# Expert stage of a two-block network: scatter, gather and turning at a change of expert, in one unit or in three

## The chip, the cores and the metric

The kernel is written in Bass and runs on one core of one Trainium2 chip. The metric is the device time of one execution in microseconds (us). The kernel before took 3509.97 us in the median of 3 runs (3504.43 to 3512.90). The engines are named as in the profile: PE (TensorE; PEld its weight loads), DVE (VectorE), ACT (ScalarE), POOL (GpSimd), SP (SyncE, which issues the weight transfers).

## The reference

The reference runs a block of depth 2 with neighbourhood attention, a bidirectional RWKV-7 and a convolution side by side, and then a second block of depth 2. Only one part of it matters here, the mixture of experts in the second layer of the first block: 256 tokens of width 1024, 8 SwiGLU experts of hidden width 3584, and each token goes to the two experts with the largest router logits, weighted by the softmax of the two.

```python
def _swiglu(h, w_gate, w_up, w_down):
    return (jax.nn.silu(h @ w_gate) * (h @ w_up)) @ w_down

    logits = (xt @ router).astype(jnp.float32)
    top_logit, top_e = lax.top_k(logits, TOP_K)
    gates = jax.nn.softmax(top_logit, axis=-1)
    ...
    y = jnp.zeros_like(xt).at[s_tok].add(yb[dest] * s_gate[:, None].astype(xt.dtype))
```

Everything is float32.

## The kernel before, in words

**Units.** The weights are cut into parts of 128 x 2048 float32 (1 MB). SP loads them, in the order of their use, into a ring of 6 slots; the load of a part waits until the part six before it has been used (`x_used`). An expert has 14 units of 256 hidden columns. A unit `U` takes three parts: two for its gate and up product, one for its down product. Float32 products are made of three matmuls: each operand is split into a high part (rounded, fp32r) and a low part (the rest). The high half of a weight part is made by ACT (`split`, line 1914), the low half by DVE (`split`, line 1984), which waits for ACT's; PE waits for DVE's (`wl_ok`). ACT has three buffers for high halves.

**The body of a unit** works on two units at once. On PE: first half of the product of unit U+1 (line 1828, 12 matmuls of 512 columns), two transposes of unit U's hidden values (`turn`, line 1836), second half of the product of U+1 (line 1828, 12), `down` of U (line 1849, 12, summed over the whole expert in banks 4 and 5). On ACT: silu of U (line 1932), split, split, the high half of the turned hidden values (line 1938), split. In the first unit of an expert the finished sums of the last expert are copied out between the two splits (`sums_out`, line 1927). On DVE: the product of silu and up (`hid`, line 1999), split, split, the low half of the turned hidden values (line 2003), split. Each engine works strictly in its written order; the order between engines is set by counting semaphores.

**A change of expert.** Tokens are picked by matmuls with one-hot matrices. For expert e there are four pieces of work:
- `choose(e)`, DVE (lines 1962 and 1964): builds the two one-hot matrices, `pick_` for gathering and `send` (with the gates) for scattering, 128 x 128 each for two token tiles.
- `gather(e)`, PE (line 1861): 16 float32 products of 128 columns (32 matmul records) into banks 6 and 7; ACT copies them out as the high half `xg_high` (line 1918), DVE makes the low half `xg_low` (line 1989).
- the turning of `send` on PE (line 1866): two transposes into bank 6, once DVE's subtraction has released it (`xcop`); ACT copies them to `sent` (line 1921).
- `scatter(e)`, PE (line 1876): 8 products of 256 columns from the expert's sums `ysb` through `sent` into banks 6 and 7, in four steps; `add(e)`, DVE (line 1973), adds each step to the tokens, and steps 2 and 3 wait for the adds of 0 and 1.

In `over_units` the first unit of an expert is unrolled, then come all four pieces (`static_part`), then 6 trips of a loop over two units, then one unrolled unit. So PE does unit 0, `scatter(e-1)`, `gather(e+1)`, the turning of `send`, unit 1. ACT does unit 0, the copies of gather and of `send`, unit 1. DVE does unit 0, `choose(e+1)`, `add(e-1)`, the subtraction, unit 1. Expert 0 has no scatter before it, expert 7 no gather. The whole is wrapped in a loop over passes; the tokens of these inputs need one pass.

Of the kernel before, what the change touches and what calls it, by code (L numbers as in the profile page):

```python
# [28 lines left out]
RING = 6  # L29
# [129 lines left out]
def build(nc, parts, xt_in, ct_in, con_in, par1_in, par2_in, lora_in, gate2_in, router_in, bias_in,  # L159
# [1456 lines left out]
    def experts(l, normed):  # L1616
# [134 lines left out]
        met, go = S("pass_met"), S("pass_go")  # L1751
        N, n_units = N_EXP * FFE_UNITS, FFE_UNITS
        base = stream["put"] - stream["skew"]
        trips = (n_units - 2) // 2
        pair_bank, turn_bank = (lambda U: bank(U % 2)), (lambda U: bank(2 + U % 2))
        pair_of = lambda U: 3 * U + 1 if U else 2
        down_of = lambda U: 3 * U + 5 if U < N - 1 else 3 * N
        assert trips * 2 + 2 == n_units and 3 * n_units % RING == 0

        def passes_of(eng):  # L1760
            return eng.value_load(passes[0:1, 0:1], min_val=1, max_val=2)
# [15 lines left out]
        @block.sync  # L1777
        def _(sp):
            sp.wait_ge(S("phase_met").h, 4 * phase["n"])
            sp.wait_ge(used.h, stream["put"])  # L1780
            with sp.Fori(0, passes_of(sp)) as p:
                def load(n, i=None, wait_for=None):

                    if wait_for is not None:
                        sp.wait_ge(x_used.h, wait_for)
                    src = parts[base + n, :, :] if i is None else \
                        parts[bass.ds(i * RING + (base + n), 1), :, :].rearrange("a p n -> p (a n)")
                    sp.dma_start(slots[:, n % RING, :], src).then_inc(x_loaded[n % RING].h, 16)
                for n in range(2):
                    load(n)  # L1790
                for e in range(N_EXP):
                    n0 = 2 + 3 * n_units * e
                    for n in range(n0, n0 + 3):
                        load(n, None, n - RING + 1 if n >= RING else None)
                    with sp.Fori(0, trips) as i:
                        for n in range(n0 + 3, n0 + 9):
                            load(n, i, i * RING + (n - RING + 1))
                    for n in range(n0 + 3 * (n_units - 1), n0 + 3 * n_units - (2 if e == N_EXP - 1 else 0)):
                        load(n, None, n - RING + 1)
                leave(sp, p)  # L1800

        def over_units(eng, e, body, static_part):


            body(e * n_units, 0, 1)
            static_part(e)
            with eng.Fori(0, trips) as i:
                for j in range(2):
                    body(e * n_units + 1 + j, i, trips)
            body((e + 1) * n_units - 1, 0, 1)  # L1810

        @block.tensor
        def _(pe):
            with pe.Fori(0, passes_of(pe)) as p:
                def take(n, i):
                    pe.wait_ge(wl_ok.h, i * RING + (n + 1))
                    return high[:, n % 3, :], low_slots[:, n % RING, :]

                def product(U, n, i, which):

                    e = (U // n_units) % 2
                    wh, wl = (v3(w, KT // 2) for w in take(n, i))
                    if which == 0:
                        pe.wait_ge(ac.h, i * 2 + (U + 1))
                    for j in range(KT // 2):
                        k = which * (KT // 2) + j
                        for g, (x, w) in enumerate(((xg_high[e], wh), (xg_high[e], wl), (xg_low[e], wh))):
                            mm = pe.matmul(pair_bank(U), x[:, k, :], w[:, j, :],  # L1828
                                           start=k == 0 and g == 0, stop=k == KT - 1 and g == 2)
                    mm.then_inc(x_used.h, 1)  # L1830

                def turn(U, i):

                    pe.wait_ge(hp.h, i * 2 + (U + 1))
                    for j in range(2):
                        mm = pe.transpose(turn_bank(U)[:, j * P:(j + 1) * P], hid[:, U % 2, j * P:(j + 1) * P],
                                          C("ident"))
                    mm.then_inc(ht.h, 1)

                def down(U, n, i, times):  # L1840
                    u = U % n_units
                    wh, wl = (v3(w, 2) for w in take(n, i))
                    pe.wait_ge(ac.h, i * 2 + (U + 3))
                    if u == 0 and U:
                        pe.wait_ge(summed.h, U // n_units)
                    for j in range(2):
                        for half in range(2):
                            for g, (h, w) in enumerate(((hid_high, wh), (hid_high, wl), (hid_low, wh))):
                                mm = pe.matmul(bank(4 + half), h[:, U % 2, j * P:(j + 1) * P],  # L1849
                                               w[:, j, half * 512:(half + 1) * 512],  # L1850
                                               start=times == 1 and u == 0 and j == 0 and g == 0,
                                               stop=times == 1 and u > 0 and j == 1 and g == 2, skip_group_check=True)
                    mm.then_inc(x_used.h, 1)

                def gather(e):
                    pe.wait_ge(picked.h, e + 1)
                    if e >= 2:
                        pe.wait_ge(added.h, 4 * (e - 1))
                    for k in range(KT):
                        for tt in range(2):  # L1860
                            mm = pe.matmul(bank(6 + k // 4)[:, (k % 4) * P:(k % 4 + 1) * P], htok[:, tt, k * P:(k + 1) * P],  # L1861
                                           pick_[e % 2][:, tt, :], start=tt == 0, stop=tt == 1)
                    mm.then_inc(gathered.h, 1)
                    pe.wait_ge(xcop.h, e + 1)
                    for tt in range(2):
                        mm = pe.transpose(bank(6)[:, tt * P:(tt + 1) * P], send[e % 2][:, tt, :], C("ident"))
                    mm.then_inc(turned.h, 1)

                def scatter(e):
                    pe.wait_ge(summed.h, e + 1)  # L1870
                    pe.wait_ge(tcop.h, min(e + 2, N_EXP))
                    for f in range(4):
                        if f >= 2:
                            pe.wait_ge(added.h, 4 * e + f - 1)
                        for m in range(2 * f, 2 * f + 2):
                            mm = pe.matmul(bank(6 + f % 2)[:, (m % 2) * LAT:(m % 2 + 1) * LAT], ysb[:, m * P:(m + 1) * P],
                                           sent[e % 2], start=True, stop=True)
                        mm.then_inc(scat.h, 1)

                gather(0)  # L1880
                product(0, 0, 0, 0)
                product(0, 1, 0, 1)

                def body(U, i, times):
                    n = 2 + 3 * U
                    if U < N - 1:
                        product(U + 1, n, i, 0)
                        turn(U, i)
                        product(U + 1, n + 1, i, 1)
                        down(U, n + 2, i, times)  # L1890
                    else:
                        turn(U, i)
                        down(U, n, i, times)

                def own_part(e):
                    if e:
                        scatter(e - 1)
                    if e + 1 < N_EXP:
                        gather(e + 1)
                for e in range(N_EXP):  # L1900
                    over_units(pe, e, body, own_part)
                scatter(N_EXP - 1)
                leave(pe, p)

        @block.scalar
        def _(act):
            with act.Fori(0, passes_of(act)) as p:
# [8 lines left out]
                def gathered_out(e):  # L1916
                    act.wait_ge(gathered.h, e + 1)
                    act.activation(xg_high[e % 2].rearrange("p k s -> p (k s)"), banks[:, 6 * 512:8 * 512], ACT.Copy)\
                        .then_inc(xh_ok.h, 1)
                    act.wait_ge(turned.h, e + 1)  # L1920
                    act.activation(sent[e % 2], bank(6)[:, 0:LAT], ACT.Copy).then_inc(tcop.h, 1)

# [15 lines left out]
                    act.activation(hid_high[:, U % 2, :], turn_bank(U)[:, 0:256], ACT.Copy).then_inc(hh.h, 1)  # L1938
                    split(3 * U + 5, i)

                def own_part(e):
                    if e + 1 < N_EXP:
                        gathered_out(e + 1)
                gathered_out(0)
                for m in range(3):
                    split(m, 0)
                for e in range(N_EXP):
# [5 lines left out]
        def _(dve):  # L1953
            keyed = S("key_moved")
            with dve.Fori(0, passes_of(dve)) as p:
# [48 lines left out]
                                      ALU.subtract).then_inc(ac.h, 1)  # L2004
                    split(3 * U + 5, i)

                def own_part(e):
                    if e + 1 < N_EXP:
                        choose(e + 1)
                    if e:  # L2010
                        add(e - 1)
                    if e + 1 < N_EXP:
                        gathered_low(e + 1)
                for e in range(N_EXP):
                    over_units(dve, e, body, own_part)
# [458 lines left out]
```

## Time and profile before

| | |
|---|---|
| median of 3 runs | 3509.97 us |
| profiled execution | 3507.41 us, span 3505.6 us |
| PE busy over the span | 3069.0 us (88%) |
| DVE, ACT busy | 2121.2 us (61%), 1555.0 us (44%) |
| mean granted TensorE clock | 0.918 |
| expert units | first silu at 1710.0, last at 2749.1 us |
| DVE waiting for ACT's split, line 1984 | 103.0 us in 207 waits |
| PE waiting for DVE before line 1866 | 19.0 us in 8 waits |

In the rows below the times of an execution are counted from the start of the span. A row of a timeline gives start, length, engine, line, operation, what it writes and reads, how many instructions are merged in it, and in brackets how long its engine was idle before it and who ended that. Matmuls are pipelined, so the rows of PE overlap somewhat; distances from start to start are safer than lengths. The instructions of ACT and DVE overlap by about 0.1 us in the same way.

### The profile page before, as it was taken

Reading aid. Unit: us, or ns where it says so; the run is one execution under the profiler, and the core shown is the slowest. Engines: PE = TensorE matmul, PEld = TensorE weight load, DVE = VectorE, ACT = ScalarE, POOL = GpSimd, SP = SyncE. Lnnn points to the kernel's source line nnn. Section 1 sums busy time; section 2 is a strip of 40 time slices with the busy share of each in tenths; the row PEclk is TensorE's granted clock in tenths of the full one; section 3 lists DMA queues with packets and bytes.
Section 4 is the critical chain, followed back from the end, with each engine's and each line's share of the span. In section 5 each row is a group of like instructions: output and inputs, shape, how many; then the busy total and the mean of one; then the engine's idle time right before and its main releaser. Section 6 shows DMA issues by size and latency. Waiting matters only on the chain.

```text
span 3505.6 us, 55996 instructions
## 1 busy us (share of the span) xinstructions
PE 3069.0 (88%) x23354; PEld 2555.7 (73%) x23354; DVE 2121.2 (61%) x2470; ACT 1555.0 (44%) x1810; POOL 0.2 (0%) x4
## 2 busy tenths in 40 slices
PE   6998499699998894775799999999999789998999
PEld 3863277489998761665687787787788667996699
DVE  3365522554445366225588888788888645764576
ACT  2223321334334234112576676676677524453453
POOL 0000000000000000000000000000000000000000
PEclk9996699899999997888899999999999878998799
DMA  6210065235454210000598898798899422542253
GB/s 257 84 60 0 19 219 193 85 132 186 170 183 151 101 49 6 2 3 1 215 369 314 312 371 312 305 371 312 313 370 351 194 84 93 184 172 97 74 190 122
DMA packets 86197, 616.06 MB, mean 176 GB/s; under 512 B 9592, under 2 KB 11264, under 8 KB 12032
## 3 DMA queue, kind: packets, MB, share of 16 engines
q1 hardware_dynamic: 82656, 601.92, 45.8%
q10 hardware_dynamic: 3360, 11.50, 0.9%
q8 instruction: 142, 2.33, 0.3%
q14 instruction: 39, 0.32, 0.0%
HBM read 612.33 MB, written 1.05 MB: 175 GB/s over the span
## 4 chain that ended last, share of the span: by engine, by line
PE 76%; DVE 14%; PEld 3%; ACT 3%; issue 1%; DMA 1%; PEldq 1%; ACTq 0%; DVEq 0%; POOLq 0%
PE banks L1828 17%; PE banks L983 14%; PE banks L635 10%; PE banks L1849 9%; PE banks L1017 6%; PE banks L1372 4%; PEld banks L635 3%; PE banks L794 2%; PE banks L771 2%; PE banks L489 1%; DVE arena L692 1%; PE banks L783 1%; PE banks L1861 1%; DVE arena L1512 1%; DVE arena L1599 1%
## 5 line engine op out<-in xcount | busy, mean ns | idle before, releaser
L1984 DVE TENSOR_TENSOR ring_split<-ring,arena_split 128x2048 fp32r<-128x2048 f32 x336 | 769.0, 2291 | 114.1 <-ACT arena_split L1914 103.0
L1914 ACT ACTIVATE arena_split<-ring 128x2048 fp32r<-128x2048 f32 x336 | 643.6, 1919 | 46.2 <-PE banks L1849 46.2
L1828 PE MATMUL banks<-arena_split 128*128 128x512 f32 x1792 | 607.4, 401 | 12.9 <-DVE ring_split L1984 12.9
L304 DVE TENSOR_TENSOR ring_split<-ring,arena_split 128x2048 fp32r<-128x2048 f32 x174 | 398.0, 2290 | 354.7 <-ACT arena_split L298 354.7
L1828 PEld LDWEIGHTS banks<-arena_split 128*128 128x128 f32 x1792 | 341.0, 190 | 88.7 <-DVE ring_split L1984 15.3
L298 ACT ACTIVATE arena_split<-ring 128x2048 fp32r<-128x2048 f32 x174 | 331.7, 1909 | 165.1 <-DVEq L235 56.1
L983 PE MATMUL banks<-mix_split,ring_split 128*128 128x256 f32 x1408 | 397.8, 283 | 0.0
L983 PE MATMUL banks<-mix_split,arena_split 128*128 128x256 f32 x1408 | 393.7, 280 | 1.9 <-DVE ring_split L304 1.6
L983 PE MATMUL banks<-h_split,arena_split 128*128 128x256 f32 x1408 | 395.1, 281 | 0.0
L1828 PE MATMUL banks<-ring_split,arena_split 128*128 128x512 f32 x896 | 355.6, 397 | 0.0
L635 PE MATMUL banks<-h_split,arena_split 128*128 128x256 f32 (+1 forms) x848 | 290.3, 342 | 68.9 <-DVE mix_split L451 68.9
L635 PE MATMUL banks<-mix_split,arena_split 128*128 128x256 f32 (+1 forms) x848 | 287.8, 339 | 43.2 <-DVE ring_split L304 16.5
L1849 PE MATMUL banks<-arena_split 128*128 128x512 f32 x896 | 295.8, 390 | 1.0 <-DVE arena_split L2003 1.0
L983 PEld LDWEIGHTS banks<-mix_split,arena_split 128*128 128x128 f32 x1408 | 265.3, 188 | 5.2 <-issue 2.7
L983 PEld LDWEIGHTS banks<-mix_split,ring_split 128*128 128x128 f32 x1408 | 265.0, 188 | 0.0
L983 PEld LDWEIGHTS banks<-h_split,arena_split 128*128 128x128 f32 x1408 | 264.1, 188 | 0.2 <-issue 0.2
L635 PEld LDWEIGHTS banks<-h_split,arena_split 128*128 128x128 f32 x848 | 167.6, 198 | 88.6 <-DVE ring_split L304 72.1
L1017 PE MATMUL banks<-arena_split 128*128 128x256 f32 x1280 | 227.9, 281 | 0.0
L635 PEld LDWEIGHTS banks<-mix_split,arena_split 128*128 128x128 f32 x848 | 167.2, 197 | 64.1 <-issue 28.5
L635 PE MATMUL banks<-mix_split,ring_split 128*128 128x256 f32 (+1 forms) x592 | 203.5, 344 | 0.0
L1849 PEld LDWEIGHTS banks<-arena_split 128*128 128x128 f32 x896 | 168.3, 188 | 40.2 <-issue 3.2
L1017 PEld LDWEIGHTS banks<-arena_split 128*128 128x128 f32 x1280 | 195.6, 188 | 0.0
(311 smaller groups left out, 4667.4 us busy)
## 6 DMA issues: line engine op xcount, KB each, us to landing
ring<-parts SPq DMA_DIRECT2D x574, 1024.0 KB, 4.8
arena<-bias ACTq DMA_DIRECT2D x2, 2048.0 KB, 9.2
x_buf<-xt ACTq DMA_DIRECT2D x1, 2048.0 KB, 23.8
constants<-con ACTq DMA_DIRECT2D x1, 2025.0 KB, 12.6
out<-x_buf ACTq DMA_DIRECT2D x1, 1024.0 KB, 4.8
arena<-lora ACTq DMA_DIRECT2D x2, 256.0 KB, 2.8
arena<-gate ACTq DMA_DIRECT2D x2, 256.0 KB, 3.5
arena<-sgw ACTq DMA_DIRECT2D x2, 256.0 KB
```

The source lines that it names most:

```text
L298: act.activation(high[:, m % depth, :], slots[:, n % RING, :], ACT.Copy).then_inc(w_high.h, w_high.one(times))
L304: dve.tensor_tensor(low_slots[:, n % RING, :], slots[:, n % RING, :], high[:, m % high.shape[1], :].bitcast(F32), ALU.subtract).then_inc(w ...
L635: mm = pe.matmul(o, left, right, start=k == 0 and n == 0, stop=k == KT - 1 and n == 2)
L771: mm = pe.matmul(score_bank(i)[:, at:at + hi - lo], q[hs, tile, qc:qc + P], k[hs, k_tile(tile), lo:hi], start=True, stop=b is None)
L794: mm = pe.matmul(bank(4 + g % 2)[hs, 0:qwide], v[:, tv, vc:vc + DH], ptr[g % 2][:, t, :], start=t == 0, stop=t == len(vt) - 1)
L983: mm = pe.matmul(bk[:, j * 256:(j + 1) * 256], w[:, k, j * P:(j + 1) * P], x[:, k, c0:c0 + 256], start=k == 0 and n == 0, stop=k == KT - 1 ...
L1017: mm = pe.matmul(y(t), w[:, j, t * P:(t + 1) * P], h[:, U % 2, j * 256:(j + 1) * 256], start=False, stop=False, skip_group_check=True)
L1372: mm = pe.matmul(out[h, i, :], left[h, i, :], right[h, i, :], start=True, stop=True)
L1828: mm = pe.matmul(pair_bank(U), x[:, k, :], w[:, j, :], start=k == 0 and g == 0, stop=k == KT - 1 and g == 2)
L1849: mm = pe.matmul(bank(4 + half), h[:, U % 2, j * P:(j + 1) * P], w[:, j, half * 512:(half + 1) * 512], start=times == 1 and u == 0 and j = ...
L1914: act.activation(high[:, m % 3, :], slots[:, m % RING, :], ACT.Copy).then_inc(wh_ok.h, 1)
L1984: dve.tensor_tensor(low_slots[:, m % RING, :], slots[:, m % RING, :], high[:, m % 3, :].bitcast(F32), ALU.subtract).then_inc(wl_ok.h, 1)
```

## The change

The unrolled opening of an expert has three units instead of one, and the loop 5 trips instead of 6. The four pieces are divided: `scatter` (with `choose` and `add` on DVE) stands behind unit 0, `gather` with its copy and its subtraction behind unit 1, the turning of `send` with its copy behind unit 2. The function `gather` loses its second half to a new function `turn_send`, and ACT's `gathered_out` loses its own to `sent_out`. SP's loads are the same, cut differently into unrolled and looped ones. The `stop` flag of `down` moves to the last unit of an expert.

```diff
+        opening = 3
-        trips = (n_units - 2) // 2
+        trips = (n_units - opening - 1) // 2
...
         def over_units(eng, e, body, static_part):
-            body(e * n_units, 0, 1)
-            static_part(e)
+            for u in range(opening):
+                body(e * n_units + u, 0, 1)
+                static_part(e, u)
             with eng.Fori(0, trips) as i:
                 for j in range(2):
-                    body(e * n_units + 1 + j, i, trips)
+                    body(e * n_units + opening + j, i, trips)
             body((e + 1) * n_units - 1, 0, 1)
...
-                                               stop=times == 1 and u > 0 and j == 1 and g == 2, skip_group_check=True)
+                                               stop=u == n_units - 1 and j == 1 and g == 2, skip_group_check=True)
...
                     mm.then_inc(gathered.h, 1)
+
+                def turn_send(e):
                     pe.wait_ge(xcop.h, e + 1)
                     for tt in range(2):
                         mm = pe.transpose(bank(6)[:, tt * P:(tt + 1) * P], send[e % 2][:, tt, :], C("ident"))
...
-                def own_part(e):
-                    if e:
+                def own_part(e, u):
+                    if u == 0 and e:
                         scatter(e - 1)
-                    if e + 1 < N_EXP:
+                    if u == 1 and e + 1 < N_EXP:
                         gather(e + 1)
+                    if u == 2 and e + 1 < N_EXP:
+                        turn_send(e + 1)
...
+                def sent_out(e):
                     act.wait_ge(turned.h, e + 1)
                     act.activation(sent[e % 2], bank(6)[:, 0:LAT], ACT.Copy).then_inc(tcop.h, 1)
...
-                def own_part(e):
-                    if e + 1 < N_EXP:
+                def own_part(e, u):
+                    if u == 1 and e + 1 < N_EXP:
                         gathered_out(e + 1)
+                    if u == 2 and e + 1 < N_EXP:
+                        sent_out(e + 1)
...
-                def own_part(e):
-                    if e + 1 < N_EXP:
+                def own_part(e, u):
+                    if u == 0 and e + 1 < N_EXP:
                         choose(e + 1)
-                    if e:
+                    if u == 0 and e:
                         add(e - 1)
-                    if e + 1 < N_EXP:
+                    if u == 1 and e + 1 < N_EXP:
                         gathered_low(e + 1)
```

## Rows read from the trace of the kernel before

**Rows 1.** Windows: stretch and length, busy time of each engine, granted clock, DMA share, GB/s.
```profile
1875.00:1965.00 90.00, 90.00 (x404) 73.58 (x403) 80.09 (x53) 67.15 (x54) 0.00 (x0) 1.00 0.96 372
1980.40:2002.60 22.20, 18.47 (x90) 14.69 (x89) 12.97 (x17) 9.66 (x9) 0.00 (x0) 0.92 0.38 142
```
**Rows 2.** Timeline of ACT: silu of the last unit of expert 1, first of 2.
```profile
1960.75 0.39 ACT L1932 ACTIVATE arena<-banks 128x256 f32<-128x256 f32 x1 [0.56 <-PE banks L1828]
...
1969.24 0.38 ACT L1932 ACTIVATE arena<-banks 128x256 f32<-128x256 f32 x1 [0.57 <-PE banks L1828]
```
**Rows 3.** Timeline of PE, the change in expert 2.
```profile
1980.40 3.99 PE L1876 MATMUL banks<-arena 128*128 128x256 f32 x16
1985.45 3.81 PE L1861 MATMUL banks<-arena 128*128 128x128 f32 x32 [1.06 <-DVE x_buf L1973]
1991.63 0.44 PE L1866 MATMUL banks<-constants,arena 128*128 128x128 f32 x2 [2.37 <-DVE arena_split L1989]
...
1996.94 0.50 PE L1828 MATMUL banks<-arena_split 128*128 128x512 f32 x1 [0.19 <-DVE ring_split L1984]
...
2002.57 0.39 PE L1828 MATMUL banks<-arena_split 128*128 128x512 f32 x1
```
**Rows 4.** Timeline of ACT, the same change.
```profile
1989.30 1.02 ACT L1918 ACTIVATE arena_split<-banks 128x1024 fp32r<-128x1024 f32 x1 [12.13 <-PE banks L1861]
...
1992.39 0.38 ACT L1932 ACTIVATE arena<-banks 128x256 f32<-128x256 f32 x1
1992.65 3.71 ACT L1914 ACTIVATE arena_split<-ring 128x2048 fp32r<-128x2048 f32 x2
...
2000.09 0.39 ACT L1932 ACTIVATE arena<-banks 128x256 f32<-128x256 f32 x1 [1.10 <-PE banks L1828]
```
**Rows 5.** Timeline of DVE, the same change.
```profile
1979.99 0.60 DVE L1962 TENSOR_SCALAR arena<-constants,arena 128x128 f32<-128x128 f32 x2
1981.46 1.74 DVE L1973 SCALAR_TENSOR_TENSOR x_buf<-banks,modv,x_buf 128x256 f32<-128x256 f32 x4 [0.88 <-PE banks L1876]
...
1994.60 4.49 DVE L1984 TENSOR_TENSOR ring_split<-ring,arena_split 128x2048 fp32r<-128x2048 f32 x2 [1.37 <-ACT arena_split L1914]
```
**Rows 6.** Timeline of PE, the change in expert 7, which has no gather.
```profile
2645.17 3.99 PE L1876 MATMUL banks<-arena 128*128 128x256 f32 x16
2648.81 0.58 PE L1828 MATMUL banks<-arena_split 128*128 128x512 f32 x1
...
2652.66 0.50 PE L1828 MATMUL banks<-arena_split 128*128 128x512 f32 x1 [0.53 <-DVE ring_split L1984]
...
2658.27 0.39 PE L1828 MATMUL banks<-arena_split 128*128 128x512 f32 x1
```
**Rows 7.** Timeline of PE, the change in expert 0, which has no scatter.
```profile
1720.19 3.84 PE L1861 MATMUL banks<-arena 128*128 128x128 f32 x32
...
1737.32 0.39 PE L1828 MATMUL banks<-arena_split 128*128 128x512 f32 x1
```
**Rows 8.** Windows, first and last of the five stretches of lowered clock.
```profile
1726.80:1730.20 3.40, 3.40 (x10) 2.64 (x10) 1.26 (x2) 3.33 (x4) 0.00 (x0) 0.50 0.03 5
2392.40:2395.80 3.40, 3.40 (x10) 2.58 (x9) 2.03 (x2) 3.40 (x2) 0.00 (x0) 0.50 0.00 0
```
**Rows 9.** Waits of the expert stage: total us, times, longest us.
```profile
PE banks L1866 <- DVE arena_split L1989: 19.0, 8, 2.4
```
**Rows 10.** Timeline of PE: second product behind the change, experts 3, 4 and 6.
```profile
2129.61 0.50 PE L1828 MATMUL banks<-arena_split 128*128 128x512 f32 x1 [1.79 <-DVE ring_split L1984]
...
2262.25 0.50 PE L1828 MATMUL banks<-arena_split 128*128 128x512 f32 x1 [1.80 <-DVE ring_split L1984]
...
2529.07 0.50 PE L1828 MATMUL banks<-arena_split 128*128 128x512 f32 x1 [1.76 <-DVE ring_split L1984]
```
**Rows 11.** Timeline of ACT, expert 4: silu of units 1 and 2.
```profile
2257.69 0.38 ACT L1932 ACTIVATE arena<-banks 128x256 f32<-128x256 f32 x1
...
2266.97 0.39 ACT L1932 ACTIVATE arena<-banks 128x256 f32<-128x256 f32 x1 [3.22 <-PE banks L1828]
```

More of the change, by code:

```diff
@@ L1757, in experts @@
         down_of = lambda U: 3 * U + 5 if U < N - 1 else 3 * N
-        assert trips * 2 + 2 == n_units and 3 * n_units % RING == 0
+        assert trips * 2 + opening + 1 == n_units and 3 * n_units % RING == 0
         def passes_of(eng):
@@ L1792, in _ @@
                     n0 = 2 + 3 * n_units * e
-                    for n in range(n0, n0 + 3):
+                    for n in range(n0, n0 + 3 * opening):
                         load(n, None, n - RING + 1 if n >= RING else None)
                     with sp.Fori(0, trips) as i:
-                        for n in range(n0 + 3, n0 + 9):
+                        for n in range(n0 + 3 * opening, n0 + 3 * opening + 6):
                             load(n, i, i * RING + (n - RING + 1))
@@ L1880, in _ @@
                 gather(0)
+                turn_send(0)
                 product(0, 0, 0, 0)
@@ L1939, in body @@
                     split(3 * U + 5, i)
-                def own_part(e):
-                    if e + 1 < N_EXP:
+                def own_part(e, u):
+                    if u == 1 and e + 1 < N_EXP:
                         gathered_out(e + 1)
+                    if u == 2 and e + 1 < N_EXP:
+                        sent_out(e + 1)
                 gathered_out(0)
+                sent_out(0)
                 for m in range(3):
```

## The prediction

> **What bounds the kernel now.** I read the expert stage in windows first. Away from a change of expert PE is busy for all of 90 us, at full granted clock, with the DMA engines at 0.96 [rows 1]. One unit takes 8.49 us there, from silu to silu [rows 2], and that is PE's own pitch: nothing else ends late. Around a change of expert (22.2 us) PE is busy for 18.47, and DMA falls to 0.38 because the ring is full [rows 1]. So only what PE does or waits for around a change can pay.
>
> The timeline of PE at the change in expert 2 shows what that is [rows 3]. I count from the start of scatter (1980.40) to the first product of the unit after next (2002.57): 22.17 us, of which 8.49 are the unit in between, so 13.68 us are extra. Of them PE works 3.64 on scatter (in expert 7 from 2645.17 to the next product at 2648.81 [rows 6]), some 3.7 on gather and 0.3 on turning `send`: 7.64. The other 6.04 are three gaps and what goes with them. The gap of 1.06 is gather waiting for the last `add`. The gap of 2.37 is the turning of `send` waiting for ACT's copy and DVE's subtraction. The third stands before the second product of the next unit: with the clock full it is 1.76 to 1.80 (experts 3, 4, 6 [rows 10]). In expert 2 it shows as 0.19 only because PE ran the first product at half clock and so reached the wait later.
>
> That third gap is the one to understand. ACT works in program order: `sent` copy, then silu (1992.39), then the split of the next weights (1992.65) [rows 4]; DVE's half follows at 1994.60 [rows 5], PE's product at 1996.94. It comes from small copies queued ahead of silu and split, and it arises wherever such a copy waits for PE to finish a piece that stands behind `down`.
>
> **The change, part by part.** The instructions are the same in number and shape; they change places. I walk the three opening units (1, 2, 3 of the new order) for experts 1 to 6.
>
> *Unit 1: scatter alone before it.* This order already runs in expert 7, which has no gather [rows 6]: from scatter 2645.17 over a gap of 0.53 (DVE finishes `add` before it splits) to the next unit's product at 2658.27, 13.10, extra 4.61. `choose` stands ahead of `add` here and not in expert 7, but it ends at 1980.59, before the first add can start at 1981.46 [rows 5]. The gap of 1.06 is gone, since gather follows a whole unit later. Bounds: 4.2 (all of `add` hidden) to 5.7 (0.53 grows to the old 1.06 and a half more).
>
> *Unit 2: gather before it.* Count from gather's start. ACT's copy starts 3.85 later (1985.45 to 1989.30) and takes 1.02 [rows 3, 4]. Behind it in ACT's order now stand silu and the split, no longer the `sent` copy. Rows of ACT overlap by about 0.1 (silu's 0.38, the split 0.26 later), so silu starts at 4.78 and the split at 5.04. DVE's subtraction is over by 6.2 (PE's wait on it ends at 1991.63 [rows 3]), and `hid`, 0.4 long, by 6.6. Its split starts 1.95 after ACT's (1992.65 to 1994.60), at 6.99, and PE's second product 2.34 after that (1994.60 to 1996.94), at 9.33; from there to the next unit 5.63 (1996.94 to 2002.57). Sum 14.96, less 8.49: extra 6.47. PE itself is ready at about 6.9: 3.7 for gather, and 3.2 for one product and the turn of `hid` (1991.63 to 1996.94 is 5.31, less 0.3 for turning `send` and the 1.79 that expert 3 waits at full clock [rows 10]). So a gap of 2.4 stands here. The old wait for the subtraction is not removed: PE no longer waits for it directly, but for the split that is queued behind it on ACT and DVE. Bounds: 3.8 (no gap) to 7.5 (1 us more on ACT).
>
> *Unit 3: the turning of `send` before it.* It finds its input long done. But its `sent` copy still waits on ACT for PE, with silu and the split behind it, so this is the old sequence from 1991.63 to 2002.57, 10.94, extra 2.45, with the old gap of about 1.8 at full clock. Bounds: 0.3 to 3.
>
> Sum 4.61 + 6.47 + 2.45 = 13.53 against 13.68: 0.15 less, in six changes -0.9 us. Expert 0 has gather and no scatter: today 1720.19 to 1737.32 is 17.13, extra 8.64 [rows 7]; after, 6.47 + 2.45 = 8.92, so +0.3. Expert 7 and the last scatter stay. The order of waits on SP's queue stays too: each load still waits for the use of the part six before it, and at a change DMA has time to spare. Shorter loops (five trips for six), longer unrolled code and the moved `stop` flag I set at nothing: unit 0, unrolled today, takes the same 8.49 as looped ones [rows 2]. Should fetching more code cost, bound it by one gap of 0.53 in each of seven changes, 4 us; should it gain, by nothing seen.
>
> **The clock.** In today's order half clock is mostly free. It comes five times between experts 0 and 5, each about 3.4 us long at half speed, which is the level of 1.2 GHz [rows 8], and falls on the product that would wait for the split anyway. In expert 4 alone it comes behind the third gap, where nothing covers it: silu to silu is 9.28 there [rows 11], against 7.70 in expert 2 (1992.39 to 2000.09 [rows 4]), 1.58 more. In the new order every half-clock stretch is uncovered: behind unit 2's gap PE has a product and `down` to run (5.63) before anything waits, behind unit 3's gap steady units. How often it comes I take from counts. The gap of 2.37 stands in eight places [rows 9]; in the seven behind a `down`, it was followed by a low stretch at once in experts 0, 1, 2 and 5, 4 of 7. Of the three gaps of 1.76 to 1.80 at full clock one was [rows 10]. The 0.53 was not. That gives 7 x 4/7 + 7 x 1/3 = 6.3 stretches of 1.58, +10.0 us; expert 4's own 1.58 is spent today: -1.6.
>
> The table "Why this matters for your kernels" on the page TensorE: Matmul & The Clock Gate of the Trainium skill warns only of idle gaps longer than any of these. By it the +10.0 would be zero, which is rival 2 below. The trace differs: the clock fell right behind 1.80 us of idle, so I go by the counts.
>
> **Sum.** The profiled execution took 3507.4 us. -0.9 + 0.3 - 1.6 + 10.0 = +7.8 gives 3515.2. It lies 2.6 under the median of the runs, 3510.0, and so I say 3517.8, rounded 3518: 0.2% slower. A difference under about 0.3% (10.5 us) can't be told from none.
>
> **Rivals.**
> 1. *The gaps vanish.* If ACT and DVE ran ahead far enough for their copies to hide, all but PE's work would go: 6 x 6.04 + (8.64 - 4.0) + 1.6 = 42 us, 3465 (3468 by the median). For it: the gap of 2.37 was a direct wait and is moved beside a product. Against: ACT has nothing queued ahead of its copy and must take silu and split after it. If only one kind of gap goes in seven changes, it is -2.2 - 16.8 + 3.6 (the 2.4) or -2.2 - 12.6 + 6.3 (the 1.8), 3495 to 3502 by the median. Together 0.12.
> 2. *The clock stays up at these gaps.* Then -0.9 + 0.3 - 1.6 = -2.2: 3505, by the median 3508. For it: three of seven gaps of 2.37 and two of three of 1.8 passed so, and PE has whole products on both sides of them now. 0.17.
> 3. *Slower: each gap costs its half clock.* Place: units 2 and 3, the gap before the second product; price 1.58 for each of 14, 22.1; with -2.2 that is +19.9, 3527 (by the median 3530). It decides over my forecast's sum of 0.3% from 8 stretches of the 14: (10.5 + 2.2) / 1.58. For it: four of seven of the longer kind already. Gaps longer than walked work the same way. 0.21.
> 4. *The forecast*, 4 to 8 stretches, 3514 to 3521: 0.50.
>
> From these cases: faster than 0.3% 0.11 (rival 1); slower 0.29 (rival 3 and the top edge of the forecast); same 0.60. The range, 3501 to 3530, leaves out the large gain and little above rival 3.
>
> **What would show it.** In experts 1 to 6: PE meets no wait between scatter and the next product; about 0.5 before unit 1's second product; about 2.4 before unit 2's, put down to DVE's split; about 1.8 before unit 3's; the turning of `send` waits for nothing. Silu to silu over the whole change stays near 13.7 above three units where the clock is full, and each stretch of half clock adds 1.6 to it. I am wrong if unit 2's gap is under 1 us, if the clock rows show fewer than 3 or more than 9 low stretches between experts 0 and 6, or if stages behind the experts change.

## The result and the profile after

The changed kernel takes 3517.36 us in the median of 15 runs (3508.95 to 3523.65), the kernel before 3509.87 in runs beside them: ratio 1.0023, 95% interval [1.0015, 1.0031]. In later runs it was 3522.31 against 3509.34, 1.0030 [1.0012, 1.0047]. So it is slower by 0.2 to 0.3%, about as forecast (3518). The prediction held that less than 0.3% can't be told from none; with this many runs both intervals stand clear of 1.

The timeline of PE at the change in expert 2 (start, length, operation, idle time before it and its releaser) answers to [rows 3]. Lines have moved: scatter is L1880, gather L1863, the turning of `send` L1870, products L1830. The view of scatter was taken up to 1989.0, so its last matmul is not in the row.

```profile
1985.52 3.77 PE L1880 MATMUL banks<-arena 128*128 128x256 f32 x15
...
1993.01 0.50 PE L1830 MATMUL banks<-arena_split 128*128 128x512 f32 x1 [0.51 <-DVE ring_split L1996]
...
1998.62 3.73 PE L1863 MATMUL banks<-arena 128*128 128x128 f32 x32
...
2007.88 0.50 PE L1830 MATMUL banks<-arena_split 128*128 128x512 f32 x1 [2.37 <-DVE ring_split L1996]
...
2015.08 0.38 PE L1870 MATMUL banks<-constants,arena 128*128 128x128 f32 x2
...
2020.34 0.50 PE L1830 MATMUL banks<-arena_split 128*128 128x512 f32 x1 [1.89 <-DVE ring_split L1996]
...
2025.94 0.39 PE L1830 MATMUL banks<-arena_split 128*128 128x512 f32 x1
```

Gather and the turning of `send` start without a wait now. But each opening unit has a gap before its second product, all three put down to DVE's split: 0.51, 2.37 and 1.89 us. ACT's timeline of the same units shows why, and answers to [rows 4]; below it stands DVE's in unit 2:

```profile
2002.39 1.03 ACT L1925 ACTIVATE arena_split<-banks 128x1024 fp32r<-128x1024 f32 x1 [7.67 <-PE banks L1863]
2003.32 0.38 ACT L1941 ACTIVATE arena<-banks 128x256 f32<-128x256 f32 x1
2003.58 3.71 ACT L1921 ACTIVATE arena_split<-ring 128x2048 fp32r<-128x2048 f32 x2
...
2015.49 0.38 ACT L1930 ACTIVATE arena<-banks 128x256 f32<-128x256 f32 x1 [6.12 <-PE banks L1870]
2015.77 0.38 ACT L1941 ACTIVATE arena<-banks 128x256 f32<-128x256 f32 x1
2016.04 3.71 ACT L1921 ACTIVATE arena_split<-ring 128x2048 fp32r<-128x2048 f32 x2
```
```profile
2003.45 1.22 DVE L2001 TENSOR_TENSOR arena_split<-banks,arena_split 128x1024 fp32r<-128x1024 f32 x1 [5.77 <-ACT arena_split L1925]
...
2005.53 4.49 DVE L1996 TENSOR_TENSOR ring_split<-ring,arena_split 128x2048 fp32r<-128x2048 f32 x2 [0.52 <-ACT arena_split L1921]
```

The reader is to see ACT idle for 7.67 us in front of the copy of gather and for 6.12 us in front of the copy of `send`, with silu (L1941) and the splits (L1921) queued right behind each. In unit 2 they could have run before: the product that silu reads had left PE by 1995.9. They wait because of their place.

Windows (busy time of PE, PEld, DVE, ACT, POOL, then granted clock, DMA share, GB/s) answer to [rows 1] and [rows 8]: the change of three units from behind scatter on, and a low stretch (granted clock 0.50, which is the level of 1.2 GHz) behind unit 2's gap and one behind unit 3's.

```profile
1989.20:2028.20 39.00, 34.22 (x160) 27.69 (x159) 27.24 (x22) 19.63 (x17) 0.00 (x0) 0.96 0.62 226
2008.90:2012.20 3.30, 3.30 (x9) 2.58 (x8) 3.30 (x3) 0.47 (x1) 0.00 (x0) 0.50 0.16 62
2558.40:2561.80 3.40, 3.40 (x9) 2.63 (x9) 3.40 (x3) 0.52 (x1) 0.00 (x0) 0.50 0.38 161
```

PE is busy through both low stretches, on products and `down`, so each costs work and not waiting. There are nine, all in experts 1 to 6: six at unit 2's gap (they begin between its last 0.5 us and 1.2 us behind it), three right behind unit 3's. Before there were five in experts 0 to 5, four of them over a product that would have waited anyway.

To compare whole changes I use ACT's silu. From the silu of unit 0 to that of unit 4, less 4 x 8.49, is what a change costs (a little more than the prediction's count on PE: 13.90 against 13.68 in expert 2 of the kernel before).

| kernel | per change, clock full | with half clock uncovered | median us | ratio to before |
|---|---|---|---|---|
| before | 13.82 to 13.90 | 15.44 (expert 4) | 3509.9 | 1 |
| changed | 13.6 (gap filled, below) | 15.16 to 16.68, six of six | 3517.4 | 1.0023 |

The profiled execution of the changed kernel took 3519.96 us, 12.6 more than that of before. Of this 2.1 lie ahead of the first silu and -0.4 behind the last, both in unchanged code, and 10.9 between them. Those are nine low stretches of 1.5 us (the six changes sum to 95.2, less 6 x 13.6 = 13.6), less expert 4's 1.6 of before and some 1.5 that the order itself gives in six changes. That makes 10.5; the other 0.4 lie in expert 0 and behind unit 4's silu.

### The profile page after: what moved, and what is told of

The parts are those of the page before. It is cut to its first block, busy times and chain, and to the rows that moved or that the text cites. A ratio compares the mean times of both kernels' runs of the same rounds, so it can differ in the third digit from the quotient of the medians.

```text
span 3518.2 us, 55644 instructions
## 1 busy us (share of the span) xinstructions
PE 3075.5 (87%) x23354; PEld 2559.7 (73%) x23354; DVE 2118.3 (60%) x2470; ACT 1551.8 (44%) x1810; POOL 0.2 (0%) x4
## 4 chain that ended last, share of the span: by engine, by line
PE 75%; DVE 15%; PEld 3%; ACT 3%; issue 2%; DMA 1%; PEldq 0%; DVEq 0%; ACTq 0%; POOLq 0%
PE banks L1830 16%; PE banks L983 14%; PE banks L635 10%; PE banks L1851 9%; PE banks L1017 6%; PE banks L1372 4%; PEld banks L635 3%; PE banks L771 2%; PE banks L794 2%; DVE ring_split L1996 1%; PE banks L489 1%; PE banks L783 1%; DVE arena L692 1%; DVE arena L1512 1%; PE banks L1863 1%
## 5 line engine op out<-in xcount | busy, mean ns | idle before, releaser
L1921 ACT ACTIVATE arena_split<-ring 128x2048 fp32r<-128x2048 f32 x336 | 642.8, 1919 | 45.2 <-PE banks L1851 45.2
L1830 PE MATMUL banks<-arena_split 128*128 128x512 f32 x1792 | 613.8, 405 | 39.7 <-DVE ring_split L1996 39.7
L1830 PEld LDWEIGHTS banks<-arena_split 128*128 128x128 f32 x1792 | 343.7, 192 | 118.4 <-DVE ring_split L1996 45.2
L1830 PE MATMUL banks<-ring_split,arena_split 128*128 128x512 f32 x896 | 357.9, 399 | 0.0
```

The lines of the kernel that those rows point to most:

```text
L1830: mm = pe.matmul(pair_bank(U), x[:, k, :], w[:, j, :], start=k == 0 and g == 0, stop=k == KT - 1 and g == 2)
L1921: act.activation(high[:, m % 3, :], slots[:, m % RING, :], ACT.Copy).then_inc(wh_ok.h, 1)
```

## The experiments

The theory: ACT and DVE take their work in written order, and a small copy that waits for a piece of PE work standing behind `down` holds up silu and the first split of the next unit. This makes the gaps, wherever the pieces stand, and behind the gaps the clock falls where nothing covers it. The rivals: the gaps come from DVE having too much to do, or from the longer unrolled code; the loss is not the clock's. The first four kernels ran on one chip (before: 3508.14, 3497.74 to 3518.36), the other four on another (before: 3509.34, 3496.40 to 3517.36).

**1. The copies of gather one step later.** `own_mid` is run inside the body of an unrolled unit, behind the first split.

```diff
                     split(3 * U + 3, i)
+                    mid()
                     split(3 * U + 4, i)
...
-                    if u == 1 and e + 1 < N_EXP:
-                        gathered_out(e + 1)
+                def own_mid(e, u):
+                    if u == 2 and e + 1 < N_EXP:
+                        gathered_out(e + 1)
```

(In the same way DVE's `gathered_low` moves.)

> Order of the changed kernel, but ACT's copy of the gathered tokens and DVE's subtraction stand one step into unit 2, behind silu (or hid) and the first split, instead of ahead of them. Theory (the queue order on ACT and DVE makes the gap of 2.4 us before unit 2's second product): that gap goes in all seven changes, 7 x 2.4 = 17, and with it the 6 low stretches that followed it, 6 x 1.5 = 9; near 3491 us, with the gap of 1.9 in unit 3 left. Rival A (PE's gap is only moved, since DVE still has 1.2 us more to do than the unit has room for): a gap of over 1 us before unit 2's down or the next product, 3500 or more. Rival B (the gap comes from PE's own work or from fetching code): 3517 as the changed kernel.

Measured: 3481.92 us, ratio 0.9933 [0.9916, 0.9950]. The gap in unit 2 is gone in all seven changes, the one in unit 3 is still 1.89, and a change costs 10.94 to 10.98, 2.65 less. DVE's timeline in unit 2 shows that it had the room:

```profile
1991.38 2.29 DVE L1998 TENSOR_TENSOR ring_split<-ring,arena_split 128x2048 fp32r<-128x2048 f32 x1 [0.29 <-ACT arena_split L1921]
1996.54 1.23 DVE L2003 TENSOR_TENSOR arena_split<-banks,arena_split 128x1024 fp32r<-128x1024 f32 x1 [2.87 <-ACT arena_split L1925]
1998.34 2.29 DVE L1998 TENSOR_TENSOR ring_split<-ring,arena_split 128x2048 fp32r<-128x2048 f32 x1 [0.58 <-ACT arena_split L1921]
```

The split that unit 2's second product needs starts at 1991.38, and is done when the gathered tokens arrive (1996.54); in the changed kernel it started behind them. Both rivals fall. The profiled execution (3489.0) is close to the 3491 that was expected, the median is 9 lower. One more thing went with the gap: of the seven gaps of 1.89 in unit 3 only one (expert 0) is followed by half clock, where three were in the changed kernel and were expected to stay.

**2. The turning of `send` earlier.** PE turns it inside unit 2, ahead of `down`; ACT's copy stays where it is.

```diff
                         product(U + 1, n + 1, i, 1)
+                        mid()
                         down(U, n + 2, i, times)
...
-                    if u == 2 and e + 1 < N_EXP:
-                        turn_send(e + 1)
+                def own_mid(e, u):
+                    if u == 2 and e + 1 < N_EXP:
+                        turn_send(e + 1)
```

> Order of the changed kernel, but PE turns send inside unit 2, between the second product and down; ACT's copy stays behind unit 2, so it finds its input done. Theory: the gap of 1.9 us before unit 3's second product goes, 7 x 1.9 = 13, with the 3 low stretches behind it, 4.5; near 3500 us, with the gap of 2.4 in unit 2 left. Rival (unit 3's gap is DVE's backlog from unit 2, not the copy that waits on ACT): the gap stays, 3517.

Measured: 3492.76 us, 0.9959 [0.9941, 0.9977]. Unit 3's gap is gone, though ACT still waits 1.77 us for the turning (6.12 before); unit 2's is still 2.37; a change costs 11.42 to 11.44, and 13.0 in the two changes with a half clock. The gap went as expected; the time is 7 us lower than expected, and the half clocks are part of it. The edit does not touch the gap of 2.37, but only two of its seven places are followed by half clock, six in the changed kernel. Between the first and the last silu the profiled execution is 26.0 us shorter than that of the changed kernel, where 17.5 were expected. Unchanged code behind the last silu took 748.5 us instead of 756.1, and ahead of the first 6.3 more; on that more below.

**3. Both.**

> Both edits together. Theory: of a change only PE's own work is left beside the gap of 0.5 in unit 1; 13.6 goes to 9.2 without low stretches: 7 x 4.3 = 30 and 9 x 1.5 = 14, near 3473 us, 1% under the kernel before. Rival (the gaps reappear elsewhere, or weight transfers become the bound once PE no longer pauses): 3490 or more, with waits on the ring's loads.

Measured: 3462.16 us, 0.9884 [0.9868, 0.9900]. ACT's timeline in the same part of a change: the copy of gather (L1928) comes behind silu and the first split of its unit, and the copy of `send` (L1933) waits 0.79 us instead of 6.12.

```profile
1981.34 0.39 ACT L1944 ACTIVATE arena<-banks 128x256 f32<-128x256 f32 x1 [1.34 <-PE banks L1830]
1981.62 1.91 ACT L1924 ACTIVATE arena_split<-ring 128x2048 fp32r<-128x2048 f32 x1
1987.67 1.03 ACT L1928 ACTIVATE arena_split<-banks 128x1024 fp32r<-128x1024 f32 x1 [4.13 <-PE banks L1863]
1988.59 1.91 ACT L1924 ACTIVATE arena_split<-ring 128x2048 fp32r<-128x2048 f32 x1
...
1993.63 0.39 ACT L1933 ACTIVATE arena<-banks 128x256 f32<-128x256 f32 x1 [0.79 <-PE banks L1870]
```

Over a whole change PE is busy 26.49 of 27 us at full clock, and the DMA engines have room:

```profile
1974.00:2001.00 27.00, 26.49 (x136) 22.12 (x135) 22.83 (x19) 15.43 (x14) 0.00 (x0) 1.00 0.68 252
```

A change costs 8.63 to 8.65 (3473 us were expected, from 9.2), and in the experts there is no low stretch. No wait on a load appears. Of the 55 us under the changed kernel, 49 lie between first and last silu in the profiled executions (1050.0 and 1001.3); the unchanged code behind gives 8.6 more there.

**4. One of the three moves undone.** The turning of `send` goes back behind gather, both behind unit 1.

```diff
                     if u == 1 and e + 1 < N_EXP:
                         gather(e + 1)
-                    if u == 2 and e + 1 < N_EXP:
                         turn_send(e + 1)
```

(On ACT likewise for `sent_out`.)

> One of the three moves undone: the turning of send goes back behind gather, so both stand behind unit 1; scatter alone behind unit 0. Theory (the loss of the change is half clock that nothing covers): PE waits 2.4 before the turning and then runs the first product at half clock, which would wait for the split anyway; a change is 13.3 instead of 13.6 without low stretches, and at most 1 to 3 of 7 low stretches cost anything: 3503 to 3507 us, faster than the changed kernel by 0.3 to 0.4%. Rival (the loss comes from dividing the work over units or from the longer unrolled code): 3517 as the changed kernel.

Measured: 3508.38 us, 1.0002 [0.9989, 1.0015]: back at the kernel before, 1.4 us above the 3503 to 3507 that were expected, though clear of the 3517 of the rival. The gap of 2.37 stands before the turning again, and where half clock followed it at once (expert 2) it cost nothing: 13.37, as in expert 4 without any (13.36). But four changes are 14.93 to 14.99. There the clock fell one step later, behind the 1.89 before the second product, as in PE's and ACT's timelines of expert 3:

```profile
2135.80 0.44 PE L1870 MATMUL banks<-constants,arena 128*128 128x128 f32 x2 [2.37 <-DVE arena_split L1999]
...
2141.11 0.50 PE L1830 MATMUL banks<-arena_split 128*128 128x512 f32 x1 [1.89 <-DVE ring_split L1994]
```
```profile
2145.83 0.39 ACT L1940 ACTIVATE arena<-banks 128x256 f32<-128x256 f32 x1 [3.23 <-PE banks L1830]
```

This silu waits 3.23 us for its product, in expert 4, without half clock, 1.65. So the old order covers a half clock only in part: at once behind the 2.37 it is free, behind the 1.89 it costs its 1.6. I had allowed 1 to 3 of 7 uncovered; in the profiled execution it was 5 (expert 0 too). Between first and last silu it took 1042.5 us, against 1050.0 of the changed kernel and 1039.1 of the kernel before.

**5. The changed kernel again,** for the chip of the next three.

> The changed kernel itself, on the same chip as the next three, so that they can be read against it. 3517 us, ratio 1.002 to 1.003; 5 to 10 stretches of half clock between experts 0 and 6, all of them behind a gap of 2.4 or 1.9 us.

Measured: 3522.31 us, 1.0030 [1.0012, 1.0047]. Again nine low stretches, six at unit 2's gap and three behind unit 3's; changes cost 15.16 to 16.62.

**6. The gap filled with work of PE.** Nothing else is touched.

```diff
                         turn(U, i)
+                        mid()
                         product(U + 1, n + 1, i, 1)
...
+                def fill(e, u):
+                    if u == 2 and e + 1 < N_EXP:
+                        for _ in range(4):
+                            pe.matmul(pair_bank(e * n_units + u)[:, 0:256], C("ident"), hT[:, 0, 0:256], start=True, stop=True)
```

> The changed kernel, and PE does four more products of 256 columns (into a PSUM bank that is free then, result unused) between the turn of the hidden values and the second product of unit 2, in the middle of what was the gap of 2.4 us: 1.8 us of work, and a gap of about 0.5 is left. No wait and no other engine's order is touched. Theory (a gap of 2.4 costs its length and, in most changes, a half clock of 1.6 more behind it): the length stays, the half clock behind unit 2 goes, 6 x 1.5 = 9: 3508 us, and no low stretch directly behind unit 2's second product. Rival (the low stretches have another cause than the idle time before them, as the mix of the work): they stay, 3517.

Measured: 3509.97 us, 1.0005 [0.9991, 1.0019], 12 us under the changed kernel on the same chip. PE's timeline, and the windows right behind unit 2's gap in expert 2 and behind unit 3's in expert 3:

```profile
2002.06 1.89 PE L1911 MATMUL banks<-h_buf,constants 128*128 128x256 f32 x8
2004.60 0.50 PE L1830 MATMUL banks<-arena_split 128*128 128x512 f32 x1 [0.65 <-DVE ring_split L2001]
```
```profile
2004.80:2008.20 3.40, 3.40 (x16) 2.77 (x16) 3.40 (x3) 1.30 (x1) 0.00 (x0) 1.00 0.40 164
2148.60:2152.00 3.40, 3.40 (x9) 2.63 (x8) 3.40 (x3) 0.72 (x1) 0.00 (x0) 0.50 0.41 173
```

The second product starts no earlier (9.25 us behind the start of gather, 9.26 in the changed kernel), yet no half clock follows unit 2 in any change. Two are left, both behind unit 3's untouched gap, where there were three. A change costs 13.59 to 13.64 without one and 15.2 with one. From nine stretches to two is 7 x 1.5 = 10.5 us, and between first and last silu the profiled executions differ by 10.9 (1050.4 and 1039.4). This settles the split between the two causes: the order alone is 0.2 to 0.3 us per change better than before, and the half clocks are the whole loss.

**7. Only the unrolling.** Three opening units, five trips, all pieces behind unit 0.

```diff
-                    if u == 1 and e + 1 < N_EXP:
+                    if u == 0 and e + 1 < N_EXP:
                         gather(e + 1)
-                    if u == 2 and e + 1 < N_EXP:
                         turn_send(e + 1)
```

> Three unrolled opening units and five trips, as in the changed kernel, but all pieces stay behind unit 0, as in the kernel before. Theory (unrolling is free): 3508 us, the kernel before, 13.8 per change. Rival (fetching the longer code costs): gaps with no releaser at the changes, up to 4 us in all, 3512.

Measured: 3510.21 us, 1.0003 [0.9990, 1.0016]; a change costs 13.86 to 13.92 (15.49 once). PEld's idle time ahead of gather that no releaser explains ("issue") is that of the kernel before, 8.6 us in 6 places. So the unrolling costs nothing that shows: 1039.4 us between first and last silu against 1039.1, and the interval of the ratio allows from 4 us less to 6 us more.

**8. Scatter divided too.**

```diff
+                    if u == 0 and e:
+                        scatter(e - 1, (0, 1))        # PE, ahead of down
...
+                        scatter(e - 1, (2, 3))        # PE, behind unit 0
...
+                        add(e - 1, (0, 1))            # DVE, behind unit 0
+                    if u == 1 and e + 1 < N_EXP:
+                        choose(e + 1)
...
+                    if u == 1 and e:
+                        add(e - 1, (2, 3))            # DVE, behind unit 1's first split
```

> Both edits of the third experiment, and in addition scatter's steps 0 and 1 stand before unit 0's down and steps 2 and 3 behind it; DVE adds 0 and 1 behind unit 0, adds 2 and 3 inside unit 1 behind its first split, and choose follows behind unit 1. Theory: the gap of 0.5 in unit 1 and the 0.3 that step 2 waits for an add go in seven changes, 5 us; only PE's own 7.6 are left of each change: 3457 us. Rival (DVE has no room for the adds inside unit 1, its busy share there is about 0.9): a wait of about as much before unit 1's down, no gain over 3462.

Measured: 3454.48 us, 0.9856 [0.9834, 0.9878]: the fastest here, 1.4% under the kernel before. A change costs 7.61 to 7.65, and PE shows no gap over 0.3 us from behind unit 0 of expert 0 to the last unit of expert 7. Its two halves of scatter:

```profile
1962.93 1.89 PE L1880 MATMUL banks<-arena 128*128 128x256 f32 x8
...
1967.42 1.89 PE L1880 MATMUL banks<-arena 128*128 128x256 f32 x8
```

That is about the 7.64 of PE's own work that the prediction counted.

**The stage by itself.** The times of whole executions hold unchanged code too, which varies by several us. The profiled executions in parts, in us, with the number of low stretches in the experts:

| kernel | ahead of first silu | first to last silu | behind last silu | low stretches |
|---|---|---|---|---|
| before | 1710.0 | 1039.1 | 756.5 | 5 |
| changed | 1712.1 | 1050.0 | 756.1 | 9 |
| 1, copies of gather late | 1711.9 | 1019.2 | 756.1 | 1 |
| 2, turning early | 1718.4 | 1024.1 | 748.5 | 2 |
| 3, both | 1710.4 | 1001.3 | 747.5 | 0 |
| 4, one move undone | 1711.4 | 1042.5 | 747.4 | 6 |
| 5, changed again | 1715.0 | 1050.4 | 755.9 | 9 |
| 6, gap filled | 1711.9 | 1039.4 | 756.5 | 2 |
| 7, unrolled only | 1709.9 | 1039.4 | 756.8 | 5 |
| 8, scatter divided | 1706.2 | 994.4 | 747.6 | 0 |

## Why the prediction was right

*Unit 1.* 13.10 from scatter to the next unit's product was taken from expert 7; measured 1985.52 to 1998.62, 13.10, with the gap of 0.51. `choose` ahead of `add` cost nothing.

*Unit 2.* From gather to the second product 9.33 was walked, 9.26 measured; the gap 2.4 against 2.37. This is the step that decided: the wait that the change removes from the turning of `send` comes back through the order on ACT and DVE. Experiment 1 shows it: with the copies one step later it is gone.

*Unit 3.* 10.94 walked, 10.86 measured; gap 1.8 against 1.89. Experiment 2 shows that it is the copy and not DVE's backlog.

*Order alone.* 13.53 against 13.68 was walked; 13.6 against 13.8 to 13.9 measured by silu in experiment 6. Code and loop at nothing: experiment 7. The queue of loads at nothing: no wait on one of these loads shows among the waits of the stage.

*The clock.* Here the sizes were off, in ways that partly cancel. What half clock does was right, how often it comes was not. I had 6.3 stretches of 1.58, +10.0. In both profiled executions there were nine, six of seven places behind unit 2's gap where the counts of before had given 4/7, three of seven behind unit 3's for 1/3, at 1.5 each: 13.6. So that term was 3.6 too small for these executions, at the edge (nine) of what I had said would still fit. The medians moved by 7.5 and 13.0 us in the two sets of runs, on either side of the forecast's +7.8. In the stage both profiled executions lost 10.9 and 11.2 us. So that 3517.4 came within 1 us of 3518 is in part luck; the 3522.3 of the later runs lies outside the 3514 to 3521 that I had given to 4 to 8 stretches. What differs between executions, the count of stretches or the unchanged code, the medians don't show. Counting was the weak step: it takes the share of gaps that half clock follows as belonging to the gap's length, and experiments 1 and 2 show that it does not. Once the other gap was gone, a gap of 2.37 was followed in 2 of 7 places instead of 6, one of 1.89 in 1 of 7 instead of 3. Experiment 6 shows that half clock is the cause of the loss: filling the idle time of one gap, and nothing else, took 12 us (11 of them in the stage).

The sentence of the Trainium skill (TensorE: Matmul & The Clock Gate, "Why this matters for your kernels") that names only idle gaps of more than about 3 us as a danger to the clock does not hold here: half clock followed 12 of the 14 gaps of 2.37 us and 6 of the 14 of 1.88 to 1.90 in the two profiled executions of the changed kernel.

Rival 1, that the gaps vanish, fell for this kernel, but its size could be had: it gave 3468, 42 us under the kernel before. Experiment 3, where the copy of gather and the subtraction come later and PE turns `send` earlier, is 37.8 shorter than the kernel before between first and last silu, experiment 8 44.7; the rest of the gain of their profiled executions (3461 and 3450) lies in code that was not changed.

## What to carry to other kernels

When a piece of one engine's work is moved behind other work, move its consumers' instructions on the in-order engines as well: look at what is queued behind each waiting copy, and put the copy behind everything that is ready before it. A wait spread over several units costs hardly less (0.2 to 0.3 us of 13.8 here), and it can cost more: here an idle gap of 1.9 or 2.4 us in an otherwise dense TensorE stream was often followed by 3.4 us at 1.2 GHz (1.5 us of time), which is free only if PE would wait anyway. How often it comes can't be carried over from one order to another. A gap already in the trace, with the same queue behind it, gave the new gap's length to a tenth of a microsecond.

## What the runs showed of the hardware

In the changed kernel a gap of 1.89 us was followed by half clock at once in 3 of 7 places, one of 2.37 in 6 of 7, in both profiled executions. The same gap of 2.37 was followed in 2 of 7 places in experiment 2, that of 1.89 in 2 of 7 in experiment 6 and in 1 of 7 in experiment 1. One of 0.5 or 0.65 never was, nor the 1.06 before gather in the kernel before. Every low stretch in the changes lasted 3.4 us. Which of the gaps is followed, I can't tell from these runs; its length alone doesn't decide it.

Unchanged code behind the experts, from the last silu to the end of the span, took 755.9 to 756.8 us in six profiled executions (before, changed twice, experiments 1, 6, 7) and 747.4 to 748.5 in four (2, 3, 4, 8). Over all of it the mean granted clock was 0.88 to 0.89 in the six and 0.90 in the four. The windows from 50 to 200 us behind the last silu, of the changed kernel and of experiment 3, differ in the granted clock:

```profile
2812.00:2962.00 150.00, 128.53 (x711) 97.19 (x710) 73.26 (x141) 50.94 (x107) 0.00 (x0) 0.76 0.23 80
```
```profile
2762.00:2912.00 150.00, 128.52 (x723) 97.02 (x722) 77.79 (x151) 52.12 (x110) 0.00 (x0) 0.80 0.23 81
```

In the same 150 us the second gets 12 more matmuls done, at 0.80 instead of 0.76. In their profiled executions up to 9 us of the gain of experiments 2, 3, 4 and 8 is this and not work that their edits touched; whether it goes with the moment at which the experts end or varies from run to run is open.
